# The first four experts of a mixture start on half a gather, with part of the shared expert moved behind them; the router multiplies by token rows, GpSimd adds squares, and TensorE gets filler products

## The reference

```
mix  = hybrid_mixer(rms_norm(h))            # merged = [rms_norm(attn), rms_norm(conv)] @ w_out
h    = h + rms_norm(mix, post_mix_norm)
t    = rms_norm(h, pre_ffn_norm)
g_w, g_idx = top_1(softmax(t @ w_group_router + b))        # 4 groups
e_w, e_idx = top_2(softmax((t @ w_expert_router + b)[group g_idx]))   # 8 experts in each group
combine    = one_hot weights, 256 tokens x 32 experts
routed = sum over e of combine[:, e] * ((silu(t @ w_gate[e]) * (t @ w_up[e])) @ w_down[e])
shared = (silu(t @ w_sh_gate) * (t @ w_sh_up)) @ w_sh_down
h    = h + rms_norm(routed + shared, post_ffn_norm)
```

## Time and profile before

| | us |
|---|---|
| median of 3 runs | 936.45 |
| lowest and highest | 934.89, 937.59 |
| the profiled execution | 933.93 |
| its span | 931.8 |
| PE busy, DVE busy, ACT busy, POOL busy in it | 807.0, 489.1, 379.8, 44.0 |
| mean granted TensorE clock | 0.946 of full |

### The profile page before, as it was taken

How to read it: one execution, slowest core, us unless ns; L and a number is a source line. 1 busy time by engine, 2 the same in 40 slices (tenths; PEclk the granted TensorE clock), 3 DMA queues, 4 the chain that set the end, 5 groups by cost and what they waited for, 6 DMA issues and landing times.

```text
span 931.8 us, 13265 instructions
## 1 busy us (share of the span) xinstructions
PE 807.0 (87%) x5425; PEld 642.8 (69%) x5425; DVE 489.1 (52%) x806; ACT 379.8 (41%) x629; POOL 44.0 (5%) x108
## 2 busy tenths in 40 slices
PE   6989997896776768559999998699999999999975
PEld 5968786763443433219989885387787999999864
DVE  5786548411100120055845586955777666666655
ACT  5564548210100110046455845535445444444444
POOL 5000020010100100000000000000000000000000
PEclk9998999998988987789999998999999999999988
DMA  9941181499999999995509452054454655565001
GB/s 281 375 164 46 46 337 48 155 384 421 421 421 421 420 421 421 417 351 171 181 3 359 155 207 102 1 226 186 153 181 157 194 192 184 195 196 192 2 0 46
DMA packets 75949, 205.80 MB, mean 221 GB/s; under 512 B 5720, under 2 KB 48896, under 8 KB 63600
## 3 DMA queue, kind: packets, MB, share of 16 engines
q1 hardware_dynamic: 67406, 150.44, 45.0%
q0 software_dynamic: 8480, 54.49, 14.5%
q10 hardware_dynamic: 2, 0.00, 0.0%
HBM read 203.87 MB, written 1.05 MB: 220 GB/s over the span
## 4 chain that ended last, share of the span: by engine, by line
PE 63%; DMA 18%; DVE 11%; ACT 5%; issue 2%; SPq 0%; POOL 0%; ACTq 0%; DVEq 0%
DMA big<-in_w_gate 15%; PE ps L1935 9%; PE ps L1936 9%; PE ps L1937 9%; PE ps L1738 8%; PE ps L1740 7%; PE ps L1739 7%; PE ps L2049 4%; DMA big<-in_w_in 3%; DVE big L1597 2%; PE ps L2028 1%; DVE WL L1062 1%; ACT WH L622 1%; DVE big L1604 1%; DVE WL L1070 1%
## 5 line engine op out<-in xcount | busy, mean ns | idle before, releaser
L1070 DVE TENSOR_TENSOR WL<-big,WH 128x1024 fp32r<-128x1024 f32 x154 | 187.0, 1224 | 121.7 <-ACT WH L622 120.4
L622 ACT ACTIVATE WH<-big 128x1024 fp32r<-128x1024 f32 x154 | 160.7, 1054 | 86.2 <-PE ps L1937 85.8
L1738 PE MATMUL ps<-XH,WH 128*128 128x256 f32 (+1 forms) x640 | 188.0, 294 | 1.4 <-DVE XL L1135 0.8
L1740 PE MATMUL ps<-XH,WL 128*128 128x256 f32 (+1 forms) x640 | 183.8, 287 | 0.0
L1739 PE MATMUL ps<-XL,WH 128*128 128x256 f32 (+1 forms) x640 | 183.7, 287 | 0.0
L1738 PEld LDWEIGHTS ps<-XH,WH 128*128 128x128 f32 x640 | 124.0, 194 | 7.1 <-issue 4.6
L2049 PE MATMUL ps<-big 128*32 128x256 f32 x1024 | 79.5, 479 | 54.1 <-DMA big<-in_w_gate 33.2
L1739 PEld LDWEIGHTS ps<-XL,WH 128*128 128x128 f32 x640 | 124.2, 194 | 0.8
L1740 PEld LDWEIGHTS ps<-XH,WL 128*128 128x128 f32 x640 | 124.2, 194 | 0.0
L2049 PEld LDWEIGHTS ps<-big 128*32 128x32 f32 x1024 | 44.6, 136 | 91.1 <-issue 81.8
L1935 PE MATMUL ps<-WH,XH 128*128 128x512 f32 x240 | 95.2, 397 | 3.1 <-issue 1.1
(11 more groups left out here) (397 smaller groups left out, 1065.9 us busy)
## 6 DMA issues: line engine op xcount, KB each, us to landing
big<-in_w_in SPq DMA_DIRECT2D x35, 1024.0 KB, 9.3
big<-in_w_gate SPq DMA_DIRECT2D x16, 1024.0 KB, 16.2
big<-in_w_up SPq DMA_DIRECT2D x16, 1024.0 KB, 17.2
big<-in_w_gate POOLq DMA_DIRECT2D x16, 1024.0 KB, 19.0
big<-in_w_up POOLq DMA_DIRECT2D x16, 1024.0 KB, 20.0
big<-in_w_down SPq DMA_DIRECT2D x16, 1024.0 KB, 17.9
big<-in_w_down POOLq DMA_DIRECT2D x16, 1024.0 KB, 20.8
big<-in_w_mlp_up SPq DMA_DIRECT2D x16, 1024.0 KB, 5.5
```

The source lines that it names most:

```text
L622: s.activation(dst, src, ACT.Copy).then_inc(ev("unit_high"), 1)
L1070: v.tensor_tensor(dst, src, h.bitcast(F32), ALU.subtract).then_inc(ev("unit_split"), 1)
L1738: mm(o, h, rh, start=first, stop=False, skip_group_check=skip)
L1740: return mm(o, l, rh, start=False, stop=last, skip_group_check=skip)
```

## The change

1. **Sums of squares.** POOL adds the squares of four chunks together (`add_square`, six additions of 128 x 256), and PE sums the two results with four matmuls in one place instead of sixteen in two.
2. **Order on DVE.** `low1(u0 + 5)` of the mix (the second of two splits between the token halves) moves behind the second half.
3. **Filler products.** `keep_busy` issues matmuls whose result nobody reads: 18 of 512 columns between the two halves' turning, 4 before the router, one of 256 columns between router chunks.
4. **Router.** For each chunk and token half the tokens are the stationary operand and the router's high and low columns, now side by side in `router`, the moving one: four matmuls with 72, 36, 72 and 36 columns. The result lies in token rows, so the copy, the turning and the wait between them go; DVE adds two small operations.
5. **First quad.** `sel` of octet 0 is written in two halves. Of the 96 products of the shared gate and up 36 (unit 2's second half and unit 3) no longer stand ahead of the gather. PE gathers quad 0's tokens only and runs gate of quad 0 at once; then it gathers quad 1's tokens, runs up, the moved shared units, hidden and down of quad 0, then the gathers of the next octet, the turning, and the shared down product. The lists of ACT and DVE follow. `low1(u0 + 5)` of the shared expert comes right behind DVE's share of `xg`.
6. **Semaphores.** Four single-use semaphores become counts on shared ones (`mark`); `sact` moves to another buffer.

```
+            added = [0]
+
+            def add_square(k):
+
+                pool.wait_ge(ev("mix_square"), in_mix(k))
+                into = mix_sq(k - k % 4)
+                last = k % 4 == 3
+                ins = g.tensor_tensor(into, into, mix_sq(k), ALU.add)
+                if last:
+                    ins.then_inc(ev("mix_added"), 1)
+                else:
+                    added[0] += 1
+                    ins.then_inc(ev("square_added"), 1)
+                    pool.wait_ge(ev("square_added"), added[0])
+
             broadcast = lambda v: v.unsqueeze(0).to_broadcast([P, D])
+            pool.wait_ge(*const("rank_or"))
+            for k in (5, 1, 2, 3, 6, 7):
+                add_square(k)
             pool.wait_ge(ev("att_out"), HEADS * TT)
...
+            act.wait_ge(ev("unit_used"), u0 + 2)
+            for t in range(TT):
+                s.activation(sact[:, t, :], ps[:, 1 + t, 0:FF], ACT.Silu, scale=st(5, t)).then_inc(ev("sh_gate"), 1)
             high1(u0 + 4)
-            act.wait_ge(ev("unit_used"), u0 + 2)
-            for t in range(TT):
-                s.activation(sact[:, t, :], ps[:, 1 + t, 0:FF], ACT.Silu, scale=st(5, t)).then_inc(ev("sh_gate"), 1)
-            high1(u0 + 5)
...
+            def gathered_first(half):
+
+                act.wait_ge(ev("gathered"), 2 * half + 1)
+                for c in range(4):
+                    s.activation(xg[:, 0, c, half * SLOTS:(half + 1) * SLOTS],
+                                 ps[:, (5, 7)[half], c * SLOTS:(c + 1) * SLOTS], ACT.Copy,
+                                 scale=gain_pc[:, c:c + 1]).then_inc(ev("xg_by_scalar"), 1)
+
+            gathered_first(0)
+            high1(u0 + 5)
+            gathered_first(1)
             act.wait_ge(*mark("group_centred"))
...
-                if t == 0:
-                    low1(u0 + 4)
-                    low1(u0 + 5)
+                low1(u0 + 4 + t)
...
-            v.tensor_copy(logits_f, ps[0:GROUPS + EXPERTS, 0, 0:S]).then_inc(ev("vector_mark"), 1)
-            dve.wait_ge(*mark("logits"))
             dve.wait_ge(ev("router_loaded"), 64)
             dve.wait_ge(*mark("ffn_in_root"))
-            for t in range(TT):
-                chain(v.scalar_tensor_tensor(out=logit[:, t, :], in0=ps[:, 4, 36 * t:36 * (t + 1)], scalar=st(5, t),
+            nr = GROUPS + EXPERTS
+            for t in range(TT):
+                chain(v.scalar_tensor_tensor(out=logit[:, t, :], in0=ps[:, 3 * t, 0:nr], scalar=st(5, t),
                                              in1=b_router[:], op0=ALU.mult, op1=ALU.add))
+            for t in range(TT):
+                chain(v.scalar_tensor_tensor(out=logit[:, t, :], in0=ps[:, 3 * t, nr:2 * nr], scalar=st(5, t),
+                                             in1=logit[:, t, :], op0=ALU.mult, op1=ALU.add))
             bc = lambda x, n: x.unsqueeze(2).to_broadcast([P, TT, n])
             io = lambda n: iota_e[:, 0:n].unsqueeze(1).to_broadcast([P, TT, n])
 
@@ -1385,16 +1426,33 @@
...
-            select(0, 0, 2 * QUAD, ev("sel_ready"))
+            def select_part(b, part):
+
+                for t in range(TT):
+                    r = rank_or[:, t, part * QUAD:(part + 1) * QUAD].unsqueeze(2).to_broadcast([P, QUAD, CAP])
+                    i_ = iota_slot[:].unsqueeze(1).to_broadcast([P, QUAD, CAP])
+                    ins = v.tensor_tensor(sel[:, b, t, part * SLOTS:(part + 1) * SLOTS].rearrange("p (e s) -> p e s", e=QUAD),
+                                          r, i_, ALU.is_equal)
+                ins.then_inc(ev("sel_ready"), 1)
+
+            select_part(0, 0)
+            select_part(0, 1)
             chain(v.tensor_reduce(r_s(8)[0:1, 0:1], ps[0:1, 4, P + 2 * EXPERTS:P + 3 * EXPERTS], AX.X, ALU.max))
             v.tensor_scalar(overflow[:], r_s(8)[0:1, 0:1], CAP + 0.5, None, ALU.is_gt).then_inc(ev("vector_mark"), 1)
             low1(u0 + 4)
-            dve.wait_ge(ev("unit_used"), u0 + 4)
-            for t in range(TT):
-                dve.wait_ge(ev("sh_gate"), t + 1)
-                v.scalar_tensor_tensor(out=sact[:, t, :], in0=ps[:, (3, 0)[t], 0:FF], scalar=st(5, t), in1=sact[:, t, :],
-                                       op0=ALU.mult, op1=ALU.mult).then_inc(ev("sh_hidden"), 1)
-
+            dve.wait_ge(ev("gain_pc_loaded"), 16)
+
+            def gathered_first(half):
+
+                dve.wait_ge(ev("gathered"), 2 * half + 2)
+                for c in range(4):
+                    v.tensor_scalar(xg[:, 0, 4 + c, half * SLOTS:(half + 1) * SLOTS],
+                                    ps[:, (6, 4)[half], c * SLOTS:(c + 1) * SLOTS], gain_pc[:, 4 + c:5 + c], None,
+                                    ALU.mult).then_inc(ev("xg_by_vector"), 1)
+
+            gathered_first(0)
+            low1(u0 + 5)
+            gathered_first(1)
             def gathered(n, o, c, bank):
 
                 dve.wait_ge(ev("gathered"), n + 1)
@@ -1402,12 +1460,6 @@
...
+            def mix_sum(branch):
+
+                pe.wait_ge(ev("mix_added"), branch + 1)
+                for t in range(TT):
+                    at = 504 + 2 * branch + t
+                    last = mm(ps[:, 3, at:at + 1], mix_sq(4 * branch)[:, t * P:(t + 1) * P], ones[:, 0:1],
+                              start=True, stop=True, skip_group_check=True)
+                return last
...
-                if k in (1, 2):
-                    pe.wait_ge(ev("mix_square"), in_mix(3) if k == 1 else 8)
+                if k == 2:
                     pe.wait_ge(ev("unit_taken_by_vector"), 8)
-                    last = mix_sums(4 * (k - 1))
-                    if k == 2:
-                        last.then_inc(ev("tensor_mark"), 1)
+                    mix_sum(0)
+                    mix_sum(1).then_inc(ev("tensor_mark"), 1)
             pe.wait_ge(ev("mix_low"), in_mix(7))
...
+            def keep_busy(n, bank, width=512):
+
+                flat = router[:].rearrange("p c n -> p (c n)")
+                for _ in range(n):
+                    mm(ps[:, bank, 0:width], flat[:, 0:P], flat[:, 0:width], start=True, stop=True)
+
             def turn_rows(x, no):
 
                 for t in range(TT):
+                    if no == 0 and t == 1:
+                        keep_busy(18, 1)
...
+            nr = GROUPS + EXPERTS
             for c in range(DC):
+                if c:
+                    keep_busy(1, 1, 256)
+                else:
+                    keep_busy(4, 1)
                 pe.wait_ge(ev("turned_low"), c + 1)
-                last = triple(ps[0:GROUPS + EXPERTS, 0, 0:S], router_hi[:, c, :], router_lo[:, c, :], xh2[:, c, :],
-                              xl2[:, c, :], c == 0, c == DC - 1)
+                for t in range(TT):
+                    tk = slice(t * P, (t + 1) * P)
+                    mm(ps[:, 3 * t, 0:2 * nr], xh2[:, c, tk], router[:, c, :], start=c == 0, stop=False,
+                       skip_group_check=True)
+                    last = mm(ps[:, 3 * t, 0:nr], xl2[:, c, tk], router_hi[:, c, :], start=False, stop=c == DC - 1,
+                              skip_group_check=True)
             last.then_inc(ev("tensor_mark"), 1)
-            pe.wait_ge(*mark("logits_by_feature"))
-            for t in range(TT):
-                last = tr(ps[:, 4, 36 * t:36 * (t + 1)], logits_f[:, t * P:(t + 1) * P],
-                          ident[0:GROUPS + EXPERTS, 0:GROUPS + EXPERTS])
-            last.then_inc(ev("tensor_mark"), 1)
...
+                if c1 == 4:
+                    last.then_inc(ev("unit_used"), 1)
...
-            shared_unit(2)
-            shared_unit(3)
...
+            shared_unit(2, 0, 2)
...
+            def gather_first(half):
+
+                pe.wait_ge(ev("sel_ready"), half + 1)
+                for k in range(2):
+                    gather(0, range(4 * k, 4 * k + 4), ((5, 6), (7, 4))[half][k], SLOTS, half * SLOTS)\
+                        .then_inc(ev("gathered"), 1)
...
-            pe.wait_ge(*mark("overflow_known"))
-            for c in OCTET0:
-                gather(0, (2 * c, 2 * c + 1), 4 + c, 2 * SLOTS).then_inc(ev("gathered"), 1)
-
-            pe.wait_ge(ev("sh_hidden"), TT)
-            for f in range(2):
-                for t in range(TT):
-                    last = tr(ps[:, 2, f * S + t * P:f * S + (t + 1) * P], sact[:, t, f * P:(f + 1) * P], ident[:])
-            last.then_inc(ev("sh_turned"), 1)
+            gather_first(0)
...
+            x = lambda c: xg[:, 0, c, 0:SLOTS]
+            pe.wait_ge(ev("sh_gate"), TT)
+            pe.wait_ge(ev("xg_by_scalar"), 4)
+            pe.wait_ge(ev("xg_by_vector"), 4)
+            wait_slots(0, 0)
+            gate_or_up(0, 0, x).then_inc(ev("expert_slab_used"), QUAD)
+            pe.wait_ge(*mark("overflow_known"))
+            gather_first(1)
+            wait_slots(0, QUAD)
+            gate_or_up(QUAD, 1, x).then_inc(ev("expert_slab_used"), QUAD)
+            shared_unit(2, 2, 4)
+            shared_unit(3)
+            pe.wait_ge(ev("hidden_ready"), 1)
```

(19 more changed lines are left out.)

180 lines of the change are left out of this document (93 added, 87 removed).

## The result

The changed kernel takes 924.04 us (median, 922.65 to 925.18) beside 935.83 us of the kernel before on the same chip: a ratio of 0.9871, 95% interval 0.985 to 0.9892. It is faster by 11.8 us. The forecast was 925.7, with a range of 921 to 931.5.

A forecast was written before the change was run, and what follows sets the result against it. The expert weight stream at 421 GB/s bounds the kernel by its start and dry places. Its free flow moves from 214.7 to 204.0, gaining 10.7 us: 933.93 becomes 923.2, plus 2.5 for the median: 925.7, range 921 to 931.5.

The forecast's parts named there:

- the start of the quad stream and its dry places: Expert stage: only when the weight stream begins and whether it runs dry counts; a gain of 10.7 us.
- Sums: Ahead of the router: eight records fewer for the sums of squares on PE save 2.5 us.
- The bound of 2.04: POOL's additions of squares: each takes at most 2.04 us, and below that they cost nothing.
- the margin: POOL's last three additions end 1.6 us before PE asks; about nothing if each waits for a DVE split.
- Half 1: DVE's writing of the second token half ahead of the router: at 145.6 us, was 149.25.
- the two rules: Router's 32 narrow matmuls: issue gap gives 0.8 us for all, loading the stationary operand 3.4; the second was taken.
- the router's part: Router: of 3.7 us gained ahead of it some go to narrow matmuls and fillers, leaving 2.8 at the ranks.
- The 13 MB: Stream: slot 11 and quad 0's three batches are all delivered at 203.4 us, was 214.7.
- Handovers and clock: Rival, first quad and router: engine handovers and half clock eat half, leaving a gain of 4 to 8 us; chance 0.20.
- Half-rate fillers: Ahead of the router, within a rival of chance 0.20: fillers at half PE rate cost 3.5 us.
- the gates of quad 1 come no earlier than before: Rival: quad 0's down waits, so quad 1's gate is no earlier than 206.7; gain under 2.8 us, chance 0.05.
- POOL never held PE: Judges the slower rival: POOL's additions hold PE at the sums, over 2.8 us slower; chance 0.05.

The follow-up runs named there:

- whole_gather: Changed kernel with the second half of the first gather ahead of quad 0's gate again; 925.95 us, ratio 0.9878.
- gate1_late: Changed kernel with twelve filler products of 512 columns ahead of quad 1's gate; 924.53 us, ratio 0.9865.
- slot11_late: Changed kernel with DVE's split that frees slot 11 behind the moves of the second half gather; 926.19 us, ratio 0.9883.
- pe_sums: Changed kernel with the squares summed by PE in two places again and no additions on POOL; 924.27 us, ratio 0.9888.
- no_chunk_fill: Changed kernel without the seven 256-column fillers between router chunks, the 18 and the 4 kept; 921.74 us, ratio 0.9857.
- no_fill: Changed kernel without any filler products; 925.54 us, ratio 0.9889.
- old_router: Changed kernel with the router of the kernel before (by features, with copy and turning) and no fillers between chunks; 920.88 us, ratio 0.9855.
- gate1_early: Changed kernel with the shared down product behind quad 1's gate instead of ahead of it; 921.72 us, ratio 0.9841.
- candidate: Changed kernel without the fillers between router chunks and with the shared down product behind quad 1's gate; 923.14 us, ratio 0.9848.
- after_again: Changed kernel run once more, unchanged; 926.09 us, ratio 0.9883.
- quad_alone: Kernel before with only the half gather, the shared expert's pieces behind it and the moved slot 11 split; 928.4 us, ratio 0.9925.

## Why the prediction was right, point by point

**What bounds the kernel.** The prediction took the start of the quad stream and its dry places as all that counts. Shown from four sides: gates 0 later by 2.1 (whole_gather) cost 2.4 to 2.6 us, gates 1 later by 2.8 (gate1_late) cost 2.7 to 3.0, slot 11 later by 8.8 (slot11_late) cost 3.5, and upstream time passes on in full (pe_sums, no_chunk_fill). The stream itself gained what was forecast: the 20th, 40th and 80th MB from 160 us on arrived at 216.7, 264.1 and 359.1 instead of 227.3, 274.8 and 369.9, 10.6 to 10.8 us earlier, with attention 1.2 us late in the trace of after. That the absolute 10.7 of the forecast is met to a tenth is therefore luck: counted from attention's end it is 11.9.

**Ahead of the router.** Sums: 2.5 forecast, 2.7 measured by pe_sums. The bound of 2.04 for an addition on POOL was far: 0.74. The one that took 1.15 began while DVE split a unit. DVE's timeline of after:

```profile
106.54 0.90 DVE L1274 SCALAR_TENSOR_TENSOR sel<-big,vec,sel 128x256 fp32r<-128x256 f32 x1
...
112.87 0.47 DVE L1274 SCALAR_TENSOR_TENSOR sel<-big,vec,sel 128x256 fp32r<-128x256 f32 x1
...
121.05 1.22 DVE L1103 TENSOR_TENSOR WL<-big,WH 128x1024 fp32r<-128x1024 f32 x1 [0.78 <-ACT WH L629]
```

The addition that starts inside the split (121.73) takes 0.41 longer than its like, and the same DVE instruction takes 0.90 where it starts just behind POOL's addition of 106.43, and 0.47 alone. The Trainium skill (SBUF — State Buffer, Who interferes with whom) has the second of a GpSimd and a two-operand DVE instruction wait for the shared port, and both rows agree. No whole split's length was lost, and the margin never came into play. Half 1 was forecast 27.7 after attention and came at 27.5. The fillers: 18 in 4.39 and the turning in 1.04 were forecast as 4.2 and about 1. The prediction gave them no worth of their own, and against before they have none up to the ranks; in the kernel after, the 22 large ones are worth 3.9 us (no_fill beside no_chunk_fill).

**Router.** The narrow matmuls were forecast at 0.105 and took 0.11; the chunk 0.54, and took 0.56; the end at 152.5, and with attention's 1.2 it was 153.5. Of the two rules that the prediction weighed, the Trainium skill's on loading (TensorE: Matmul & The Clock Gate, LDWEIGHTS) holds here, and the formula on the issue gap does not describe this case: by the page's own words it is the gap of an isolated matmul, and here each one loads a new stationary operand. The ranks moved by 3.2 where 2.8 was forecast. By the forecast 3.65 us gained at half 1 shrink to 2.8; measured, 3.82 shrink to 3.2. So the prediction had the sign of the router's part right, a loss of 0.85 where 0.64 was measured. It did not say what loses: the seven fillers cost 0.8 there, and the token-row form itself gains 0.2. The expectation of old_router speaks of a step of the prediction by which the token-row form gains more than it costs; the sum above holds no such gain. The gain up to the ranks is that of the sums (2.7) and of the split order (the other 1.1 at half 1), less the 0.6.

**The first quad.** The gather took 3.74 (forecast 4.0), DVE's four moves 1.13 (1.2), the gate 3.66 (3.5). Slot 11 was forecast for 168.5 and came at 169.1, the batches for 171.0, 178.5, 187.9 and 202.4, and they came at 171.6, 179.0, 188.4 and 202.3. Counted from attention's end they are 0.6 to 1.3 us early. The 0.6 that joined last lies between the downs and quad 1's gate, where two quarter gathers of 1.99, turnings and the shared down product took 13.9 instead of 14.5.

**The stream.** The 13 MB were forecast to end at 203.4 and the next request to flow at 204.0, a hole of 0.6 us. The dip in the windows is worth 0.6. So the term was right, and closing the dip (gate1_early, candidate) moves the last down by 0.3 to 0.5. Block 2 moves by 1.35 to 1.9 with it, by the order of the last landings and the clock of the last up products, which the prediction did not have.

**The size.** From attention's end the gain is 12.8, in the forecast 10.7. 1.2 of the difference is that the batches are earlier than forecast by the count from attention. The other 0.9 appears behind the stream: the last ups start 11.1 earlier than in before (379.03 beside 390.16), not 10.7, and run 5.63 instead of 6.10 at another granted clock. The prediction has no term for that clock, and it varies from trace to trace. The two profiled spans differ by 9.5 only (931.8 and 922.3): of the 12.8, attention takes 1.2 back and the second block 2.1 (515.8 against 513.7 behind block 2). The medians differ by 11.8. The forecast of the median also put the runs 2.5 above the profiled execution, as in before; in after they lie at it (924.04 and 924.16). So the steps and the size of the mechanism were right to about 2 us, and that the median came within 1.7 us of the forecast is in part luck.

**The rivals.** Handovers and clock did not eat half: granted clock 1.00 from 142 to 206, with the idle 1.45 us ahead of quad 0's gate and 1.06 ahead of its down. In four other traces a stretch of half clock did fall there, and it cost 0.6 at the gates. Half-rate fillers did not occur. That the gates of quad 1 come no earlier than before is refuted (5.5 earlier), and POOL never held PE.

## What to carry over

Where a long stream of weights runs at the rate of the memory, look for when it starts and for every place where it runs dry; the place of one early instruction that frees a slot can be worth more than its own length, above all where other loads queue behind that slot's, and work that no one waits for belongs behind the instruction that frees a batch. Test fillers group by group: of two groups here the one that covers a pause of PE is worth 3.9 us in this kernel, and the one inside busy work costs 0.9. When single executions differ by more than the edit, count from a common event of each trace instead of comparing spans, and run the unchanged kernel once more, so that each edit has a neighbour with the same accidents.

## What the runs showed of the hardware that was not expected

**The granted clock falls on a busy TensorE too.** Each trace looked at has a half-clock stretch inside attention, behind windows in which PE has pauses (2.01 of 4.00 us busy in 66 to 70 of after). It ran from 70 to 76 us in slot11_late, whose attention ended at 116.1, and from 76 to 86 in gate1_late, whose attention ended last (120.6), with the same instructions. A second one, of some 3.4 us at the half level, stands between 152 and 158 us in four of the eight traces with all of the router's fillers, with PE busy for 2.00 of every 2.00 us before and in it (windows of after_again above). The third place is in the attention of the second block. Windows of after_again, and of before at the same distance from block 2:

```profile
555.00:565.00 10.00, 6.64 (x38) 3.69 (x34) 7.24 (x16) 7.81 (x16) 0.00 (x0) 0.67 0.08 34
565.00:575.00 10.00, 10.00 (x52) 5.65 (x50) 8.26 (x18) 4.55 (x12) 0.00 (x0) 0.50 0.01 2
...
585.00:595.00 10.00, 9.18 (x53) 5.26 (x53) 8.93 (x19) 5.08 (x13) 0.00 (x0) 0.62 0.00 0
```

```profile
568.00:578.00 10.00, 6.00 (x34) 3.63 (x36) 7.33 (x16) 8.10 (x16) 0.00 (x0) 0.73 0.02 9
578.00:588.00 10.00, 7.89 (x60) 4.58 (x59) 9.70 (x22) 4.99 (x12) 0.00 (x0) 0.93 0.00 1
```

Here before regains its clock within 20 us and after_again only after 35, and it takes 5.4 us more behind block 2 (519.1 against 513.7). The candidate has the same long stretch (521.2). In the ten microseconds in which it begins PE works 6.64 and 6.00 us, with pauses. What decides between the short and the long stretch was not found; no run here changes it on purpose.

**The same pause costs differently.** Before and quad_alone have the same pause of 4.73 us ahead of the router. Behind it the granted clocks of the windows from 148 to 156 amount to 3.4 us at the half level in before (0.85, 0.50, 0.80) and to 6.8 in quad_alone, and the ranks come 1.65 later. In before the cost stays hidden: PE's last router record ends at 155.16, when DVE is still in the split (154.21, 1.22 us) that stands ahead of its copy of the router's result.
